# The mixer's first loads issued in the convolution's last unit, and the forward state products in two PSUM places

## What is computed

```python
qk_l, v_l, o_l, zm_l, g_l, hy_l, zh_l = split_proj(hl @ w_in[l])     # and the same for the context
hm_c, hm_l = mlstm_bidirectional(ctx_in, lat_in)                      # 4 heads x 128, both directions
m_l = mlstm_output(hm_l, o_l, zm_l, mh_gain[l])
filt_l = implicit_filters(L_lat, ...)                                 # long filters, order 2
y_hy_l = hyena_mixer(hy_l, zh_l, rows, ..., filt_l, filt_bias[l])     # convolution by FFT, 512 channels
y_l = jnp.concatenate([m_l, y_hy_l], axis=-1) @ w_out[l]
new_xl = xl + gate_l[:, None] * rms_norm(y_l, post_gain[l])
```

## Time and profile before

| | |
|---|---|
| Median of 3 runs | 1684.63 us (1683.03 to 1684.9) |
| The profiled execution's own time | 1683.12 us |
| Its span, first to last instruction | 1681.3 us |
| PE busy | 1581.0 us, 94% of the span |
| DVE, ACT, POOL busy | 710.3, 673.7, 307.6 us |
| DMA over the span | 201.72 MB, mean 120 GB/s |
| Stages | project to about 911 us, hyena to about 1323, mixer to the end |

### The profile page before, as it was taken

One profiled execution on the slowest core, in us unless ns is written; L12 is line 12 of the kernel. 1 busy time (PEld: TensorE's weight loads), 2 busy tenths in 40 slices (PEclk: granted clock), 3 DMA queues, 4 the chain that ended last, 5 costly groups with the idle time before them and its releaser, 6 DMA issues. The chain is left out here.

```text
span 1681.3 us, 23549 instructions
## 1 busy us (share of the span) xinstructions
PE 1581.0 (94%) x8886; PEld 1358.3 (81%) x8886; DVE 710.3 (42%) x1123; ACT 673.7 (40%) x1371; POOL 307.6 (18%) x297
## 2 busy tenths in 40 slices
PE   7799999999999999999997799999998556999997
PEld 3788888888888888888886789999897556888886
DVE  1654420333333333010201677777675256555553
ACT  2885212342222222131111655565653256555451
POOL 1551000000000000000000021212122005665652
PEclk9899999999999999999998899999999789999999
DMA  9241521222221122121113644535353564665651
GB/s 363 75 129 50 207 76 55 75 72 75 75 74 69 75 75 95 49 100 49 47 50 147 176 123 119 166 92 169 93 145 76 169 210 157 193 206 181 202 189 51
DMA packets 128191, 201.72 MB, mean 120 GB/s; under 512 B 12555, under 2 KB 75713, under 8 KB 121190
## 3 DMA queue, kind: packets, MB, share of 16 engines
q1 hardware_dynamic: 128102, 200.52, 37.8%
HBM read 122.45 MB, written 52.86 MB: 104 GB/s over the span
## 5 line engine op out<-in xcount | busy, mean ns | idle before, releaser
L454 PE MATMUL bank<-h_hi,w_hi 128*128 128x512 f32 (+1 forms) x840 | 325.1, 387 | 0.0
L456 PE MATMUL bank<-h_hi,w_lo 128*128 128x512 f32 (+1 forms) x840 | 323.4, 385 | 0.0
L455 PE MATMUL bank<-h_lo,w_hi 128*128 128x512 f32 (+1 forms) x840 | 323.2, 385 | 0.0
L454 PEld LDWEIGHTS bank<-h_hi,w_hi 128*128 128x128 f32 x840 | 158.5, 189 | 31.2 <-issue 0.2
L456 PEld LDWEIGHTS bank<-h_hi,w_lo 128*128 128x128 f32 x840 | 158.5, 189 | 31.3
L455 PEld LDWEIGHTS bank<-h_lo,w_hi 128*128 128x128 f32 x840 | 158.7, 189 | 30.9 <-issue 0.2
L454 PE MATMUL bank<-w_hi,h_hi 128*128 128x512 f32 (+1 forms) x448 | 164.5, 367 | 0.0
L455 PE MATMUL bank<-w_lo,h_hi 128*128 128x512 f32 (+1 forms) x448 | 164.1, 366 | 0.0
L456 PE MATMUL bank<-w_hi,h_lo 128*128 128x512 f32 (+1 forms) x448 | 164.1, 366 | 0.0
L822 DVE SCALAR_TENSOR_TENSOR work<-work,coef 128x504 f32<-128x504 f32 (+1 forms) x84 | 62.3, 742 | 239.8 <-ACT work L610 239.7
L600 ACT ACTIVATE work<-bank 128x512 f32<-128x512 f32 (+1 forms) x72 | 40.4, 562 | 299.2 <-PE bank L456 299.1
(11 more groups left out here) (225 smaller groups left out, 2845.4 us busy)
## 6 DMA issues: line engine op xcount, KB each, us to landing
H<-spectrum SPq DMA_DIRECT2D x192, 128.0 KB, 2.4
stage<-in_w_in SPq DMA_DIRECT2D x18, 1024.0 KB, 5.9
s_hy<-work SPq DMA_DIRECT2D x48, 256.0 KB, 2.2
xin<-s_hy SPq DMA_DIRECT2D x8, 1024.0 KB, 5.2
kq<-s_k SPq DMA_DIRECT2D x32, 256.0 KB, 4.6
v<-s_v SPq DMA_DIRECT2D x32, 256.0 KB, 5.0
mb<-s_rows SPq DMA_DIRECT2D x32, 256.0 KB, 5.6
late<-in_x SPq DMA_DIRECT2D x16, 512.0 KB, 4.8
```

Source lines behind the costliest of these rows:

```text
L454: pe.matmul(out, lhs[0], rhs[0], start=(k == 0), stop=False)
L455: pe.matmul(out, lhs[0], rhs[1], start=False, stop=False)
L456: return pe.matmul(out, lhs[1], rhs[0], start=False, stop=(k == KD - 1))
```

## The change

The first loads of the mixer move to a class `Early`, which lays its buffers over the convolution's filter buffers (`layer` to `A2f`, brought together for that). SyncE issues them in the last group behind the H copies of the last unit and ahead of the store of y. Among them are now all eight rows of the output weights (4 MB), so there is no second half to load and no wait for `wo_low_m` ahead of chunks 9 to 17. The wait for the last store of y leaves `hyena` and stands in the mixer ahead of `load_yh(0)`. `late`, `y_lo` and `wib` now lie over the raw output weights, so their first writers wait for the low rows (`wo_low_m` or `wo_low_h`). Forward products go by turns to `psN[:, 0]` and to the two `acc` banks (`grown`); PE waits for the state update two chunks back instead of one, and the first output sum also waits for `cf_ready`. `HIGH_WO` becomes chunks 2 to 9.

```diff
-HIGH_WO = (4, 5, 6, 7, 12, 13, 14, 15)
+HIGH_WO = (2, 3, 4, 5, 6, 7, 8, 9)
+class Early:
+    def __init__(self, nc, ctx):
+        self.kq = at("kq", [P, SLOTS, HEADS, P])
+        self.v1 = at("v1", [P, SLOTS, HEADS, V1])
+        self.raw = at("wo_raw", [P, KD, D])
...
+    def load(self, sp, d, s):
+        self.load_kv(sp, s, 0)
+        sp.dma_start(self.cols[:, :, :, :].rearrange("p d w r -> p (d w r)"), s["cols"]).then_inc(self.cols_in, 16)
+        sp.dma_start(self.ident[:, :], d["ident"]).then_inc(self.ident_in, 16)
+        for dr in range(2):
+            sp.dma_start(self.wc[:, dr, :], spread(s["small"][dr, 3])).then_inc(self.wc_in, 16)
+        self.load_kv(sp, s, 1)
+        sp.dma_start(self.gain[:, :], d["gaincol"]).then_inc(self.gain_in, 16)
+        for half in range(2):
+            cut = slice(half * HEADS, (half + 1) * HEADS)
+            sp.dma_start(self.raw[:, cut], d["w_out"][:, cut]).then_inc(self.wo_in, 16)
+        self.load_kv(sp, s, 2)
+        self.load_kv(sp, s, 3)
+        sp.dma_start(self.mask[:, :, :], d["mask"]).then_inc(self.mask_in, 16)
+        for dr in range(2):
+            sp.dma_start(self.mpb[:, dr, :], spread(s["small"][dr, 2])).then_inc(self.mpb_in, 16)
...
-        acc = [ps(f"acc{c}", [P, TILE]) for c in range(2)]
+        acc = ps("acc", [P, 2, TILE])
+        grown = [psN[:, 0], acc[:, :, 0:2 * V1].rearrange("p a (b v) -> p a b v", b=2)]
...
-            for c in range(SLOTS):
-                load_kv(c)
...
-            for c in range(SLOTS, 9):
-                load_kv(c)
-            sp.dma_start(mask[:, :, :], d["mask"]).then_inc(const_in, 16)
-            for dr in range(2):
-                sp.dma_start(mpb[:, dr, :], spread(s["small"][dr, 2])).then_inc(mpb_in, 16)
-            sp.wait_ge(wo_low_m, HEADS)
-            sp.dma_start(stage_w, d["w_out"][:, KD // 2:KD]).then_inc(wo_in, 16)
-            for c in range(9, 13):
+            for c in range(SLOTS, 13):
                 load_kv(c)
...
+            sp.wait_ge(early.y_out, 16 * GROUPS)
             load_yh(0)
...
             def increments(c):
                 if c < NT - 1:
                     pe.wait_ge(kwf_ready, c + 1)
-                    if c:
-                        pe.wait_ge(cf_ready, c)
+                    if c == 0:
+                        pe.wait_ge(const_set, 1)
+                    if c >= 2:
+                        pe.wait_ge(cf_ready, c - 1)
                     for hd in range(HEADS):
-                        mm = pe.matmul(psN[:, 0, hd // 2, hd % 2, :], kw[:, c % 2, 0, hd, :], v1[:, c % SLOTS, hd, :],
+                        mm = pe.matmul(grown[c % 2][:, hd // 2, hd % 2, :], kw[:, c % 2, 0, hd, :], v1[:, c % SLOTS, hd, :],
...
                 else:
                     pe.wait_ge(wo_low_h, HEADS)
+                    pe.wait_ge(cf_ready, NT - 2)
                 out_part(range(HEADS, KD)).then_inc(hy_summed, 1)
...
-                if c == 2:
+                if c == 1:
                     scale_gain()
...
                 else:
-                    act.wait_ge(mpb_in, 32)
+                    act.wait_ge(early.mpb_in, 32)
+                    act.wait_ge(wo_low_h, HEADS)
...
+                else:
+                    early.load(sp, d, s)
                 wait_taken(sp, g, (1, "back", F_TILES - 1))
                 sp.dma_start(s["y"][:, :, g, :].rearrange("c p t -> p c t"),
                              x2[:, :].rearrange("p (c t) -> p c t", t=P)).then_inc(y_out, 16)
-                wait_count(sp, y_out, g, 16, 16)
                 if ahead:
+                    wait_count(sp, y_out, g, 16, 16)
                     load_gates(g + 1)
```

More of the change, by code:

```diff
@@ L979, with place, load_kv @@
 SLOTS = 4
-HIGH_WO = (4, 5, 6, 7, 12, 13, 14, 15)
-def mixer(nc, d, s, out):
+HIGH_WO = (2, 3, 4, 5, 6, 7, 8, 9)
+class Early:
+    def __init__(self, nc, ctx):
+        sem = sem_maker(nc, ctx)
+        self.offset = nc.sbuf_base
+        self.size = 0
+        at = lambda name, shape: self.place(nc, name, shape)
+        self.kq = at("kq", [P, SLOTS, HEADS, P])
+        self.v1 = at("v1", [P, SLOTS, HEADS, V1])
+        self.raw_offset = self.offset + self.size
+        self.raw = at("wo_raw", [P, KD, D])
+        self.cols = at("cols", [P, 2, 3, HC])
+        self.mpb = at("mpb", [P, 2, HC])
+        self.wc = at("wc", [P, 2, HC])
+        self.ident = at("ident_m", [P, P])
+        self.mask = at("mask", [P, 2, P])
+        self.gain = at("gain", [P, HEADS])
+        self.kv_in = [sem(f"kv_in{i}") for i in range(SLOTS)]
+        self.ident_in = sem("ident_in")
+        self.gain_in = sem("gain_in")
+        self.mask_in = sem("mask_in")
+        self.wc_in = sem("wc_in")
+        self.mpb_in = sem("mpb_in")
+        self.cols_in = sem("cols_in")
+        self.wo_in = sem("wo_in")
+        self.y_out = sem("y_out_h")
+    def place(self, nc, name, shape):
+        tensor = nc.alloc_sbuf_tensor_at(name, shape, F32, offset=self.offset + self.size)
+        self.size += -(-4 * math.prod(shape[1:]) // 32) * 32
+        return tensor
+    def load_kv(self, sp, s, c):
+        slot = c % SLOTS
+        sp.dma_start(self.kq[:, slot], s["k"][c]).then_inc(self.kv_in[slot], 16)
+        sp.dma_start(self.v1[:, slot, :, 0:DH], s["v"][c].rearrange("p (h v) -> p h v", h=HEADS))\
+          .then_inc(self.kv_in[slot], 16)
+    def load(self, sp, d, s):
[14 more added lines that the diff above has]
+            sp.dma_start(self.mpb[:, dr, :], spread(s["small"][dr, 2])).then_inc(self.mpb_in, 16)
@@ L985, in mixer @@
+FILTER_BYTES = 4 * (2 * HALF_T + 4 * 2 * P + N2 * P + 2 * N2 * P + 2 * (K1 // 4) * P)
+def mixer(nc, d, s, out, early):
     with ExitStack() as ctx:
@@ L999, in mixer @@
         z = late[:, 4 * D:6 * D].rearrange("p (b n) -> p b n", b=2)
[L1000 to L1004, removed]
+        raw, ident, mask, gain = early.raw, early.ident, early.mask, early.gain
         gains = sb("gains", [P, HEADS])
[L1006 to L1010, removed]
+        cols, mpb, wc = early.cols, early.mpb, early.wc
+        kq, v1 = early.kq, early.v1
         kT, qT = kq[:, 0:2], kq[:, 2:4]
-        v1 = sb("v1", [P, SLOTS, HEADS, V1])
         kw = sb("kw", [P, 2, 2, HEADS, P])
-        mb = sb("mb", [P, 2, 2, HEADS, P])
-        wib = sb("wib", [P, 2, HEADS, P])
         og = sb("og", [P, 2, HEADS, P])
         zg = sb("zg", [P, 2, HEADS, P])
-        yh = sb("yh", [P, 2, HEADS, P])
+        yh = early.place(nc, "yh", [P, 2, HEADS, P])
         h = kw[:, 0, 0]
@@ L1050, in mixer @@
         wo_low_h = sem("wo_low_h")
-        kv_in = [sem(f"kv_in{i}") for i in range(SLOTS)]
+        kv_in = early.kv_in
         k_turned = sem("k_turned")
@@ L1784, in hyena @@
         A2f = sb("A2f", [P, NQ, P])
+        assert nc.sbuf_base == early.offset + FILTER_BYTES and early.size <= FILTER_BYTES
+        x2 = sb("x2", [P, T_LAT])
+        tables = sb("tables", [P, 2, NQ, P])
+        outer = sb("outer", [P, 2 * K1])
+        back = sb("back", [K1, 2, P])
+        ident = sb("ident_h", [P, P])
+        ones = sb("ones_h", [P, P])
+        guard = sb("guard_h", [P, 1])
         sums = sb("sums", [P, P])
```

86 lines of the change are left out of this document (34 added, 52 removed).

## The result

The changed kernel took 1655.76 us in the median of four runs (1655.01 to 1656.43), the kernel before 1683.83 beside it; the ratio is 0.983, with a 95% interval of 0.9817 to 0.9844. It is 28.1 us faster. Forecast were 1653.5 us and a span 30.5 us shorter. The profiled execution has a span of 1654.7 us, 26.6 less than before.

A forecast was written before the change was run, and what follows sets the result against it. TensorE, busy 94%, was taken as the bound, with time to win only in the mixer's prologue. 4.7 + 9.8 + 13.6 + 3.4 - 1.0 = 30.5 us gave span 1650.8, written as 1653.5, range 1647 to 1662.

The forecast's parts named there:

- the signs I had set down as right: Profile signs around the mixer's prologue, such as early first memset, short value waits, high clock, last backward product near 1370.
- M: The mixer's first instruction, a GpSimd memset; forecast 4.7 us earlier because the block needn't wait for the y store.
- The rival of a block's end that waits for the store: At the convolution's end: the block still waits for the store, first mixer instruction unmoved; price 4.7 us, 1658, chance 0.08.
- Moved loads cost nothing: In the convolution's last group: 18 load issues, 6.9 MB, fit idle DMA time; cost 0, upper bound 2 us.
- M to E0: Mixer's first instruction to end of chunk 0's backward product: from 14.0 to 4.2 us, a gain of 9.8.
- The clock's term: TensorE at the mixer's start: a pause lowers its clock, costing 1.0 us, between 0 and 7.
- The rival of a cold start: At the prologue's start: TensorE's clock falls to 1.2 GHz, costing 7 us instead of 1; 1659.5, chance 0.06.
- E0 to E8: Ends of backward products of chunks 0 to 8: from 36.5 to 22.9 us, a gain of 13.6.
- E8 to E17: Ends of backward products of chunks 8 to 17: from 26.7 to 23.3 us, near the load supply, gain 3.4.
- The second place: Second PSUM place for the prologue's forward products: gives the state update a chunk more time; 3.4 us behind chunk 8.
- pace stays: Prologue chunks keep the old pace of 3 us or more; price 5.7 us, 1659.2, chance 0.10.
- Behind E17: From chunk 17's backward product to the end: 280.8 us kept, cost 0, at most 2.4.

The follow-up runs named there:

- e2_store_wait: The changed kernel with SyncE's wait for the last store of y put back at the end of the convolution; 1661.37 us.
- f3_late_apart_warm: The changed kernel with loads not needed at once put later, low weight rows kept apart, and 12 idle transposes behind the last convolution product; 1646.91 us, ratio 0.978.
- f0_again: The changed kernel, unaltered, run and profiled a second time; 1658.33 us, ratio 0.985.
- f2_late: The changed kernel with step 0's y and rows loaded among chunks 5 to 8, step 1's rows and the gates behind the queries; 1653.09 us.
- the pair at full clock: f3_late_apart_warm with forward products in one PSUM place again, 1657.32 us, beside f3_late_apart_warm itself, 1646.91 us.
- g2_before_reordered: The kernel before, with the wo_low_m wait and the load of the output weights' second half moved behind the loads of chunks 9 to 12; ratio 0.998.
- e1_one_place: The changed kernel with forward products in one PSUM place again, each waiting for the state update of the chunk before; 1660.48 us.

## Why the prediction was right, and where its terms were off

The direction and the place were right, the mechanism too but for the supply behind chunk 8, and the time lay in the range, with the second set's median of 1658.33 as well. That it came within 2.3 us of 1653.5 is in part luck: the terms' errors are 1.8 us one way and 5.7 the other. Of the signs I had set down as right three failed in the profile: no wait for values over 1.5 us (4.13), a clock of 0.9 or more from 1320 to 1326 (0.50 and 0.71), a last product near 1370 (1373.7). Of those for wrong one came true, the waits at chunks 13 and 17. By its steps:

- **M.** Forecast 4.7 us; measured 5.54 - 0.80 = 4.74. e2_store_wait gives 5.5 behind the store again. The rival of a block's end that waits for the store is out.
- **Moved loads cost nothing.** Right: the convolution's last unit didn't stretch beyond what executions differ by, and the 1302 slice has a DMA share of 0.00. The issue was not as forecast, though: SyncE took 9.52 us for the issue of `mask` alone (the row below), and was done at 1296.1 instead of 1286. It still had 20 us until the store. In the other profiles with moved loads this issue took 7.0 to 9.1 us.

```profile
1285.67 9.52 SPq L1036 DMA_DIRECT2D mask<-in_mask  x1
```

- **M to E0.** The chain was right, 4.17 to 4.20 us in seven of the profiles with the mixer's early start. The clock's term was mis-sized: taken 1.0, it is 2.2 in some executions and 0 in others. The rival of a cold start came true in kind, at 2.2 where it had 7. The row I had taken as nearest (1314, 1.00) told nothing of it; the one of 1302 did, with 0.69 behind 8 us of which PE was busy for 4.72.
- **E0 to E8.** Forecast 22.9, measured 21.9, by two errors that partly cancel. Chunks 2 and 3 took 4.8 together instead of 5.8 (chunk 2 has no backward product), chunks 4 to 6 2.66 to 2.83 each instead of 3.0, chunk 8 with its weight row 2.2 instead of 2.8. The collision of the two low rows, which I had not seen, cost 1.4 at chunk 7.
- **E8 to E17.** The failed term: forecast 23.3, measured 27.6 and 25.8. I had written that supply is late next, and divided 5.5 MB by 276 GB/s. That is a floor, not a time. A chunk's values are asked for only when the products four chunks before are done, so the queue must answer within about two chunks, 4.8 us by the pace of this stretch. The values of chunk 13 were asked for at 1349.33, behind y and rows (0.8 MB) issued from 1347.09 on, and PE stood still for them from 1353.28. The DMA issues from 1348 to 1350 show when they landed:

```profile
v<-s_v SPq DMA_DIRECT2D x1, 256.0 KB, 8.0
```

The DMAs were saturated from 1354 to 1358 and idle for half of the next four microseconds (share 1.05 and 0.48, the last but one column):

```profile
1354.00:1358.00 4.00, 0.59 (x5) 0.59 (x6) 0.48 (x2) 0.00 (x0) 0.00 (x0) 1.00 1.05 351
1358.00:1362.00 4.00, 4.00 (x24) 4.00 (x22) 1.72 (x5) 1.80 (x6) 0.00 (x0) 0.57 0.48 164
```

SyncE issued nothing between 1356.5 and 1361.1, because its next load waits for the product that PE could not yet make. Bytes over rate knows neither. The same rows show a second cost of the wait: behind it the clock is at 0.57. Against the 20.7 of f3_late_apart_warm, whose prologue runs at 1.00, the 27.6 are 5.3 of waits for values and, by difference, 1.6 that I put down to this clock; the 25.8 of f0_again, where the clock stayed at 1.00, are 4.7 of waits and 0.4. f2_late and f3_late_apart_warm show the stretch without the other loads, 21.0 and 20.7, PE's own bound. (I had also written that nine chunks behind E8 have no weight row; with `HIGH_WO` up to 9 it is eight.)
- **The second place.** I gave it 3.4 us behind chunk 8 and nothing ahead of it. It carries 4.7 ahead of chunk 8 (25.1 against 20.4 in the pair at full clock), and behind it 0 or 4.5, as the supply allows. The rival "pace stays", with what the Trainium skill says in *TensorE: Matmul & The Clock Gate*, section "HAM oscillation" (double buffering of PSUM gave another kernel nothing), is refuted for this kernel as a whole, and held behind chunk 8 for another reason than PSUM.
- **Behind E17.** 281.0 for 280.8, and within 280.0 to 282.5 everywhere. A microsecond off the prologue was a microsecond off the span, to within this scatter of 2.5.

The terms' errors: 0.8 gained in the convolution and 1.0 from E0 to E8, lost 1.2 from M to E0 with the clock, 4.3 behind E8, 0.2 at the end. In sum 3.9, the difference of the spans, 1654.7 to 1650.8.

## What to carry to other kernels

Loads of a stage's start belong into the idle DMA time of the stage before, and the gain is what is out of the stage's way; the same bytes in another order ahead of their use mostly moved the stall here (8.0 of 11.8 us in g2_before_reordered). Where loads are asked for by progress through a few slots, compare the landing time of one load under load with the time its slots give, not bytes with bandwidth, and put what is needed later behind what is needed now. Before an operation is put beside another engine's, look for a row in which both ran at once.

## What the hardware showed that was not expected

- VectorE's 128x1024 row with two SBUF inputs took 2.61 to 2.66 us beside GpSimd's in six profiles, 1.27 to 1.28 in the five profiles with the rows apart, and in e1_one_place, whose pace kept them apart.
- SyncE's issue of one DMA took 9.52 us (7.0 to 9.5 in twelve profiles) behind some 6 MB of loads issued just before, and 5.55 us behind 2 MB and rows; alone such an issue takes 0.3 to 0.6 us.
- The clock falls at different places in executions of the same program: 0.50 from 1318 in one, 0.72 from 1302 and 1.00 from 1318 in the other, 2.25 us apart in the mixer's first chunk.
